# One set of squares for a final norm and the norm behind it, and the normed residual moved into the next feed-forward

## The reference, cut to what matters

```python
def first_block(x, ..., w_ffn_gate, w_ffn_up, w_ffn_down, ln_final):
    for l in range(DEPTH):
        ...
        u = rms_norm(h, ln_ffn[l])
        h = h + (silu(u @ w_ffn_gate[l]) * (u @ w_ffn_up[l])) @ w_ffn_down[l]
    return rms_norm(h, ln_final)[:, META_END:]       # the final norm

def second_block(x, c, ...):
    mod = silu(c) @ w_ada + b_ada                    # sh1, sc1, ga1, ... nine parts
    h = rms_norm_2(x, g_pre_ff1) * (1 + sc1) + sh1   # the norm behind it
    f = swiglu(h, w1_gate, w1_up, w1_down)
    x = x + 0.5 * ga1 * rms_norm_2(f, g_post_ff1)
    ...

def rms_norm(x, g):                                  # rms_norm_2 is the same
    return x * rsqrt(mean(x * x) + 1e-6) * g
```

## Time and profile before

| | |
|---|---|
| median of 3 runs | 3220.3 us (3218.08 to 3223.06) |
| profiled execution, its own time | 3220.06 us |
| its span, first to last instruction | 3217.5 us |
| mean granted clock of PE | 0.967 of full speed |
| busy: PE, DVE, ACT, POOL | 3034.4 us (94%), 1767.5 (55%), 1015.8 (32%), 222.6 (7%) |

### The profile page before, as it was taken

How to read it: one execution, slowest core, us unless ns; L and a number is a source line. 1 busy time by engine, 2 the same in 40 slices (tenths; PEclk the granted TensorE clock), 3 DMA queues, 4 the chain that set the end, 5 groups by cost and what they waited for, 6 DMA issues and landing times.

```text
span 3217.5 us, 51830 instructions
## 1 busy us (share of the span) xinstructions
PE 3034.4 (94%) x21724; PEld 2586.9 (80%) x21724; DVE 1767.5 (55%) x3317; ACT 1015.8 (32%) x1745; POOL 222.6 (7%) x455
## 2 busy tenths in 40 slices
PE   8999999999999899999999999989999897789997
PEld 7777998999999887789897888858888464568886
DVE  4564577457566447457755756556356453553334
ACT  4655232332122246523223222233222215332221
POOL 0130222000000102122200000000000000000000
PEclk8989999999999999989999999989999998899998
DMA  5201111235443320111123545312334210122231
GB/s 176 101 15 47 50 67 59 71 135 181 144 137 112 119 79 28 47 45 64 59 80 138 183 145 170 117 49 98 110 114 172 102 32 29 53 70 102 90 100 70
DMA packets 74494, 302.47 MB, mean 94 GB/s; under 512 B 10728, under 2 KB 11112, under 8 KB 69272
## 3 DMA queue, kind: packets, MB, share of 16 engines
q1 hardware_dynamic: 57880, 230.04, 21.1%
q0 software_dynamic: 16384, 69.13, 6.0%
HBM read 288.51 MB, written 14.63 MB: 94 GB/s over the span
## 4 chain that ended last, share of the span: by engine, by line
PE 85%; DVE 7%; ACT 5%; issue 2%; DMA 1%; POOL 0%; ACTq 0%; DVEq 0%; SPq 0%
PE acc L1040 17%; PE acc L1041 17%; PE acc L1042 17%; PE acc L1302 5%; PE acc L1303 5%; PE acc L1304 5%; PE acc L1059 2%; PE acc L1205 2%; ACT temps L1709 1%; PE acc L1074 1%; DVE work L2035 1%; PE acc L1179 1%; PE acc L1533 1%; PE acc L1152 1%; PE acc L1347 1%
## 5 line engine op out<-in xcount | busy, mean ns | idle before, releaser
L1041 PE MATMUL acc<-normed_r,toep_r 128*128 128x512 f32 (+1 forms) x1824 | 642.8, 352 | 0.0
L1638 ACT ACTIVATE toep_r<-ring 128x1024 fp32r<-128x1024 f32 (+2 forms) x340 | 392.6, 1157 | 707.4 <-PE acc L1042 691.1
L2086 DVE TENSOR_TENSOR ring_r<-ring,toep_r 128x1024 fp32r<-128x1024 f32 (+2 forms) x340 | 457.9, 1348 | 261.6 <-ACT toep_r L1638 261.2
L1041 PEld LDWEIGHTS acc<-normed_r,toep_r 128*128 128x128 f32 x1824 | 344.5, 189 | 46.1 <-issue 0.2
L1040 PE MATMUL acc<-mixed_r,toep_r 128*128 128x264 f32 (+1 forms) x1056 | 342.6, 324 | 5.1 <-DVE ring_r L2086 4.4
L1040 PE MATMUL acc<-work_r,toep_r 128*128 128x512 f32 (+1 forms) x988 | 341.7, 346 | 1.5 <-DVE ring_r L2086 1.4
L1042 PE MATMUL acc<-work_r,ring_r 128*128 128x512 f32 (+1 forms) x988 | 340.9, 345 | 0.0
L1042 PE MATMUL acc<-mixed_r,ring_r 128*128 128x264 f32 (+1 forms) x1056 | 338.8, 321 | 0.0
L1040 PE MATMUL acc<-temps_r,toep_r 128*128 128x512 f32 x768 | 305.0, 397 | 24.3 <-DVE normed_r L2072 14.8
L1041 PE MATMUL acc<-work_r,toep_r 128*128 128x512 f32 (+1 forms) x880 | 307.3, 349 | 0.0
L1302 PE MATMUL acc<-residual_r,toep_r 128*128 128x264 f32 (+1 forms) x1024 | 301.8, 295 | 3.7 <-ACT toep L1818 2.1
(11 more groups left out here) (408 smaller groups left out, 5379.3 us busy)
## 6 DMA issues: line engine op xcount, KB each, us to landing
ring<-in_w_pair SPq DMA_DIRECT2D x176, 512.0 KB, 3.5
ring<-in_w_down SPq DMA_DIRECT2D x64, 704.0 KB, 4.1
ring<-in_w_gb SPq DMA_DIRECT2D x64, 640.0 KB, 3.9
extra<-in_w_ada POOLq DMA_DIRECT2D x18, 1024.0 KB, 6.2
toep<-in_w_ada POOLq DMA_DIRECT2D x18, 1024.0 KB, 6.1
ring<-in_w_tm SPq DMA_DIRECT2D x24, 512.0 KB, 4.5
ring<-in_w_out SPq DMA_DIRECT2D x24, 512.0 KB, 3.5
ring<-in_w_fm SPq DMA_DIRECT2D x20, 512.0 KB, 3.8
```

The source lines that it names most:

```text
L1041: mm(out, wh, xl[:, a:z], start=False, stop=False)
L1638: A(high(ld), slot(ld), ACT.Copy).then_inc(S["w_high"], 1)
L2086: V.tensor_tensor(low(ld), slot(ld), high(ld), ALU.subtract).then_inc(S["w_low"], 1)
```

## The change

The norm behind the final one, `b2["pre1"]`, takes its mean from the squares of h that the final norm has anyway. `norm` gets a bank, a place for its inverse, and a mark for a norm that squares nothing of its own; `b2["pre1"]` now stands ahead of `norm_final`, with its own sum TOTALW and bank 6, and `norm_final` has bank 7 and its inverse in RFINAL. While the down jobs run, DVE adds each square also with the weight of its tile (`weight` = g g + eps). The last tile's weight is put into the matrix of the mean (LASTW). PE runs the four mean matmuls together (`joint_means`). ACT takes both roots, that of `b2["pre1"]` first. DVE then makes that inverse and writes U from h with the gain `joined` = `fg(0)` g. The final norm's inverse is made inside the next feed-forward, in pair 0, and H is multiplied by it in pairs 1 to 4, two tiles each, ahead of the pair's state-space step. The six folds stand ahead of the down jobs of the second half.

```diff
+        TOTALW, RFINAL, LASTW = span(E, 0, L), span(E, L, L), cross[:, 0:P]
...
-        norm_final = norm(H, h_there, range(KT), TOKENS, "h_done", total=TMP)
-
         b2 = {}
-        b2["pre1"] = norm(H, norm_final["done"], range(KT), TOKENS)
+        b2["pre1"] = norm(H, h_there, range(KT), TOKENS, total=TOTALW, squared=False)
+        norm_final = norm(H, h_there, range(KT), TOKENS, "h_done", total=TMP, bank=7, inverse=RFINAL)
...
+            def joint_means(own, weighted):
+
+                a, z = own["pieces"][0]
+                pe.wait_ge(S["mean_read"], weighted["n"])
+                pe.wait_ge(S["weights_made"], 1)
+                pe.wait_ge(S["sq_used"], own["sq0"] + KT - 2)
+                mm(weighted["acc"][:, 0, :], mean[D], weighted["total"][:, a:z], start=True, stop=False)
+                mm(own["acc"][:, 0, :], mean[D], own["total"][:, a:z], start=True, stop=False).then_inc(S["sq_used"], 1)
+                pe.wait_ge(S["sq_ready"], own["sq0"] + KT)
+                x = SQ[(KT - 1) % 2][:, a:z]
+                mm(weighted["acc"][:, 0, :], LASTW, x, start=False, stop=True).then_inc(S["joint_mean"], 1)
+                mm(own["acc"][:, 0, :], mean[D], x, start=False, stop=True).then_inc(S["sq_used"], 1)
...
-                mean_square(norm_final)
+                joint_means(norm_final, b2["pre1"])
                 second_block()
 
             def second_block():
-                mean_square(b2["pre1"])
+                pe.wait_ge(S["mean_read"], norm_final["n"] + 1)
                 ffn(b2["ffn1"], ssm=True)
...
+                root(b2["pre1"])
                 root(norm_final)
                 act.wait_ge(S["params2_loaded"], 32)
                 A(sc["dt"], pp("step"), ACT.Exp).then_inc(S["dt_ready"], 1)
-                squares(b2["pre1"])
                 ffn(b2["ffn1"], b2["post1"], ssm=True)
...
+                    if weighted is not None:
+                        w = weighted["total"][:, a:z]
+                        if i == 1:
+                            link(V.tensor_scalar(w, n["total"][:, a:z], weight[:, 0:1], None, ALU.mult))
+                        V.scalar_tensor_tensor(out=w, in0=SQ[i % 2][:, a:z], scalar=weight[:, i:i + 1], in1=w,
+                                               op0=ALU.mult, op1=ALU.add)
...
+            def joint_weights():
+
+                g = gain("ln_final")
+                link(V.tensor_tensor(weight, g, g, ALU.mult))
+                link(V.tensor_scalar(weight, weight, EPS, None, ALU.add))
+                link(V.tensor_tensor(joined, fg(0), g, ALU.mult))
+                V.tensor_scalar(LASTW, mean[D], weight[:, KT - 1:KT], None, ALU.mult).then_inc(S["weights_made"], 1)
...
                     advance(u.loads[0])
+                    if ssm and i == 0:
+                        rinv(norm_final)
+                    if ssm and 0 < i < 5:
+                        normed_tiles(norm_final, gain("ln_final"), H, range(2 * i - 2, 2 * i))
                     if ssm:
                         ssm_step(i)
...
+                    if i >= FH and weighted is not None:
+                        folded()
+                        joint_weights()
                     for k, j in enumerate(f["down"][i // FH]):
                         if i >= FH:
-                            summed(then, k - 1)
+                            summed(then, k - 1, weighted)
...
-                normed(norm_final, gain("ln_final"), H)
-                folded()
-                normed(b2["pre1"], fg(0), U, split=b2["ffn1"]["x"])
+                normed(b2["pre1"], joined, U, split=b2["ffn1"]["x"])
                 ffn(b2["ffn1"], b2["post1"], ssm=True)
```

More of the change, by code:

```diff
@@ L319, in build @@
         ostat = cell(20)
+        weight, joined = cell(8), cell(8)
+        epsq = cell(1)
         dec = [cell(2) for _ in range(2)]
@@ L542, in build, with norm @@
         norms = []
-        def norm(src, ready, tiles, pieces, signal="u_ready", total=None):
+        def norm(src, ready, tiles, pieces, signal="u_ready", total=None, bank=6, squared=True, inverse=None):
             n = dict(total=total, n=len(norms), src=src, ready=ready, tiles=tiles, pieces=pieces,
-                     acc=PS[:, 6:6 + len(pieces), 0:pieces[0][1] - pieces[0][0]],
-                     sq0=sum(len(m["tiles"]) for m in norms), signal=signal)
+                     acc=PS[:, bank:bank + len(pieces), 0:pieces[0][1] - pieces[0][0]],
+                     sq0=sum(len(m["tiles"]) for m in norms if m["squared"]), signal=signal, squared=squared,
+                     inverse=RINV if inverse is None else inverse)
             n["done"] = [mark(signal) for _ in tiles] if signal else None
@@ L1617, in root @@
             def root(n, rinv_used=None):
-                act.wait_ge(S["sq_used"], n["sq0"] + len(n["tiles"]))
+                if n["squared"]:
+                    act.wait_ge(S["sq_used"], n["sq0"] + len(n["tiles"]))
+                else:
+                    act.wait_ge(S["joint_mean"], 1)
                 if rinv_used:
                     wait(act, rinv_used)
-                A(two(RINV, n["pieces"]), n["acc"], ACT.Sqrt, bias=epsc).then_inc(S["mean_read"], 1)
+                A(two(n["inverse"], n["pieces"]), n["acc"], ACT.Sqrt, bias=epsc if n["squared"] else epsq
+                  ).then_inc(S["mean_read"], 1)
             def squares(n, rinv_used=None):
@@ L1903, in start_lambda @@
                 A(cact, part(par, PARAMS, "c_cols"), ACT.Silu).then_inc(S["cact_ready"], 1)
-            act.wait_ge(S["constants_set"], 3)
+            act.wait_ge(S["constants_set"], 4)
             def first_block():
@@ L2033, in rinv @@
                 dve.wait_ge(S["mean_read"], n["n"] + 1)
-                r = two(RINV, n["pieces"])
+                r = two(n["inverse"], n["pieces"])
                 V.reciprocal(r, r).then_inc(S["rinv_ready"], 1)
@@ L2037, in rinv, with summed @@
                 return n["pieces"][0][0], n["pieces"][-1][1]
-            def summed(n, i):
+            def summed(n, i, weighted=None):
                 if 1 <= i < KT - 1:
@@ L2049, in normed, with normed_tiles @@
             def normed(n, g, dst, shift=None, split=None):
-                a, z = rinv(n)
-                for i, k in enumerate(n["tiles"]):
+                rinv(n)
+                normed_tiles(n, g, dst, range(len(n["tiles"])), shift, split)
+            def normed_tiles(n, g, dst, at, shift=None, split=None):
+                a, z = n["pieces"][0][0], n["pieces"][-1][1]
+                for i in at:
+                    k = n["tiles"][i]
                     ins_ = V.scalar_tensor_tensor(out=dst[:, k, a:z], in0=n["src"][:, k, a:z], scalar=g[:, i:i + 1],
-                                                  in1=RINV[:, a:z], op0=ALU.mult, op1=ALU.mult)
+                                                  in1=n["inverse"][:, a:z], op0=ALU.mult, op1=ALU.mult)
                     if shift is not None:
@@ L2102, in _, with ffn @@
             made_silu = [0]
-            def ffn(f, then, ada=None, l=0, ssm=False):
+            def joint_weights():
[4 more added lines that the diff above has]
+                V.tensor_scalar(LASTW, mean[D], weight[:, KT - 1:KT], None, ALU.mult).then_inc(S["weights_made"], 1)
+            def ffn(f, then, ada=None, l=0, ssm=False, weighted=None):
                 if f["scaled"]:
@@ L2504, in _ @@
             V.memset(epsc, EPS).then_inc(S["constants_set"], 1)
+            V.memset(epsq, EPS * EPS).then_inc(S["constants_set"], 1)
             V.memset(zerocol, 0.0).then_inc(S["constants_set"], 1)
@@ L2801, in first_block @@
                     low_tile(ly["ffn"]["x"], KT - 1)
-                    ffn(ly["ffn"], layers[1]["norm"] if l == 0 else norm_final, ada=18 * l, l=l)
-                normed(norm_final, gain("ln_final"), H)
-                folded()
-                normed(b2["pre1"], fg(0), U, split=b2["ffn1"]["x"])
+                    ffn(ly["ffn"], layers[1]["norm"] if l == 0 else norm_final, ada=18 * l, l=l,
+                        weighted=b2["pre1"] if l else None)
+                normed(b2["pre1"], joined, U, split=b2["ffn1"]["x"])
                 ffn(b2["ffn1"], b2["post1"], ssm=True)
```

2 lines of the change are left out of this document (1 added, 1 removed).

## The result

| | before | after |
|---|---|---|
| median | 3220.53 us (3218.08 to 3223.06, 4 runs) | 3198.33 us (3198.08 to 3199.45, 4 runs) |
| profiled execution, its own time | 3220.06 us | 3198.08 us |
| its span | 3217.5 us | 3196.3 us |
| mean granted clock of PE | 0.967 | 0.972 |

The ratio is 0.9932, with an interval of 0.9914 to 0.9949. The span is 21.2 us shorter where 13.6 were expected.

What follows compares the result with a forecast made beforehand. TensorE was taken to bound 85% of the chain, but two norms in series to bound the changed place. The gain of 16.2 less 2.6 for moved work gave 13.6 us, hence 3206.5 us, range 3202.8 to 3211.5.

Steps and rivals of the forecast that it cites:

- The gain at the place: Between last down matmul and next feed-forward's first matmul: eight squares, a root and an inverse leave the chain, gaining 16.21 us.
- What was added there: At the norms: extra mean matmuls, a root on ACT, folds and small products on DVE, all covered, costing nothing.
- The moved work: Next feed-forward, pairs 0 to 4: 8.7 us of moved DVE work makes PE wait once, losing 2.6 us.
- The clock behind the wait: At PE's new wait of 2.4 to 2.6 us in pair 1: the clock stays at 1.00, nothing charged.
- a sign of being wrong: Next feed-forward: a clock of 0.50 between the gate jobs of pairs 3 and 5 would make the prediction wrong.
- rival 2: At PE's new wait the clock falls, losing 2.8 us or twice that: 3209.3 to 3212.1 us; chance 0.15.
- The sum: Whole kernel: 16.2 - 2.6 = 13.6 us off the profiled 3220.06 us, giving 3206.5 us.
- The first (all is covered): Next feed-forward: the split of pair 3's gate weight comes in time, no loss: 3203.9 us; chance 0.13.
- The others: More waits, up to 3212.6 us, chance 0.09; first matmul unmoved, 3220, 0.04; slower in pairs 0 to 4, 3254, 0.03.

Runs made afterwards that it cites:

- a_const: The changed kernel with its new constant's memset set beside the weights of the squares instead of at the program's start; 3206.40 us, ratio 0.9958.
- a_delay: a_const plus an unread 128x256 copy on DVE ahead of the second layer's second gate product; 3199.57 us, ratio 0.9939.
- late: The changed kernel with the final norm's inverse in pair 3, three products in pair 4 and five in pair 5; 3194.47 us, ratio 0.9929.
- b_delay: The kernel before plus an unread 128x256 copy on DVE ahead of the second layer's second gate product; 3218.86 us, ratio 1.0000.
- b_const2: b_const unchanged, run again for a second trace; 3220.76 us, ratio 1.0002.
- b_const: The kernel before plus only the early 128x1 memset on DVE and ACT's wait for it; 3218.51 us, ratio 1.0002.
- c_before: The kernel before, unchanged, run again for a second trace; 3219.22 us.

## Why the prediction was right and wrong

**The gain at the place** was forecast as 16.21 us and is 16.21: the distance of g_0's first matmul from the last down matmul, by their starts, went from 25.99 to 9.78. One inverse and one root went off the chain, as the earlier trace rows let it be read.

**What was added there** cost nothing, as forecast. The Exp stands at 2124.83, which is 1.9 us ahead of the first high tile where 1.6 were forecast. The folds and small products shrank DVE's idle time before the first down sum from 3.44 to 1.42 us, by 2.0 where 2.1 to 2.3 were forecast.

**The moved work.** On the axis of the changed kernel (21.49 us earlier) the high part of u_2 was forecast for 2157.06 and began at 2156.93, its low part 2158.18 against 2158.00, that of g_3 2166.95 against 2166.77. PE waited 2.06 us where about 2.4 were forecast, once, and there was no second wait. The whole, 2.6 us, is 2.57 in a_const, where nothing of the clock is mixed in.

**The clock behind the wait** is the first step that failed: the prediction charged nothing for it, from one row with a wait of 2.25 us and a clock of 1.00. The changed kernel shows 0.50 for 3.4 us behind waits of 2.06 and 2.12 in its two traces, a_delay the same behind 2.12, and a_const 1.00 behind one of 2.10. It is what the prediction itself named as a sign of being wrong. So the length of a wait alone does not decide it, at about 2 us. The price, 1.55 us, is about half of the 2.8 in rival 2, whose stretch was taken as 6.0 us. The Trainium skill ("TensorE: Matmul & The Clock Gate", section "HAM oscillation — how this bites in real kernels"), which the prediction weighed and set aside here, says that a wait that is long enough makes the next burst start cold. The waits of its example are longer than those here, so it doesn't settle them: the changed kernel shows a cold start, a_const and the wait in the earlier trace rows show none.

**The sum** is the step that put the time below the range. It took the profiled 3220.06 us, subtracted what the change does at its place, and left all other stages as they were. The other stages did not stay. Of the 8.4 us between the forecast and the profiled 3198.08, 3.8 went with the stretch near 1367 and 3.9 came behind the place, most of them with the stretch near 2733; the changed kernel lacks both stretches. Another 1.5 are how the two executions began, 0.8 lie outside the span, and the clock behind the wait took 1.55 back. The prediction didn't count the 128x1 memset at the start among the parts of the change, and I know of no row of before from which its effect could be read. With the clock of before in those stages the forecast holds: in a_const, the change with the memset moved, the span counted from the first gate product (1333.37) is 13.7 us shorter than before's, and 13.6 were forecast. That its time, 3206.40 us, lies within 0.1 of the 3206.5 is luck in part: it began 0.8 us later than the trace of before and has 0.7 less outside the span.

**The rivals.** The second (the clock falls at the wait) came true in the changed kernel at half its price. The first (all is covered) is what late does by another order. The others did not happen. That a stretch of the clock elsewhere in the program might come or go was not among the cases, so the range had no room for it.

**What stays open:** what in how an execution begins shifts all that follows by some 2 us between two traces of before; why one memset at the start makes DVE begin an instruction 0.46 us instead of 0.11 behind its input some 1340 us later (in seven traces of seven with the memset at the start, and not once in the six without); and what sets the stretch near 2720 to 2733. The unread copy is not quite another means than the memset: in all nine traces with a late product the product is entry 1855 among DVE's recorded instructions, counted from 0, and 1854 in the four with a punctual one. The lateness by place and that by the copy's own 0.29 us can't be told apart in b_delay and a_delay. What the lateness did to the clock doesn't hang on that.

## What to carry to other kernels

When a step is taken off a chain that stands twice, read the gain as the distance of the same step in its two places, and follow what is moved through each engine until some wait has room for it: that gave the two terms here, 16.21 and 2.6 us, to 0.1. Place moved work by the slack of the stage it goes into: the same 8.7 us of DVE work cost 7.6 us in one lump, 4.1 in portions from pair 0 on (each with what the clock did), and nothing from pair 3 on. A forecast of a 0.5% gain needs room for stretches at half clock elsewhere in the program, each worth 3 to 4 us here; list those that the trace of before has, and compare two kernels stage by stage before a difference of their times is put down to the change. Take distances between two rows of one trace and not times from its start: the two traces of before differed by 2.05 us at the same row, and by 0.05 in the distance from there to the last down matmul.

## What the runs showed of the hardware

- A shift of 0.3 to 0.4 us of a single DVE instruction decides over 13.7 us at 1.2 GHz some 30 us later, worth 3.8 us (787.6 against 791.4 us from row to row). It did so with a memset and with a copy and in both kernels, in eight of eight traces in which the clock had fallen 227.8 us before the first product, and not in the one with 229.6.
- What such a shift gains can be lost again: in b_delay and b_const2 a later stretch grew from 13.7 us to 30.7 and 41.0, and the medians stayed that of before.
- About equal waits of PE went either way: 2.06 and twice 2.12 us were followed by 1.2 GHz, 2.10 and 2.25 us by 2.4 GHz.
- Two executions of one kernel can differ by 1.3 to 2.1 us long before the changed place: b_const and b_const2, the same program, had the first gate product at 1334.72 and 1333.42, before and c_before at 1332.55 and 1330.50.
